# Expert gate tables: one-hot products on TensorE replaced by indirect adding transfers into zeroed device memory

## The reference, cut to what matters

```python
s1 = einsum('thd,hnd->thn', qp[..., :half], sub_k1)     # 8 heads, 128 keys each
s2 = einsum('thd,hnd->thn', qp[..., half:], sub_k2)
v1, i1 = top_k(s1, 16); v2, i2 = top_k(s2, 16)
vals, flat = top_k((v1[..., :, None] + v2[..., None, :]).reshape(T, 8, 256), 16)
experts = e1 * 128 + e2                                 # e1, e2: looked up in i1, i2 by flat
gates = softmax(vals)                                   # 16 per token and head
hid = gelu(einsum('cd,chkd->chk', x, u_tab[experts]))
out = einsum('chk,chkd->cd', gates * hid, v_tab[experts])
```

## Time and profile before

| | |
|---|---|
| median of 3 runs | 2321.66 us (2321.47 to 2322.29) |
| the profiled execution, span from first to last instruction | 2321.0 us |
| PE / DVE / ACT / POOL busy | 2284.5 / 1685.9 / 1213.7 / 475.5 us |
| granted TensorE clock, mean | 0.997 |
| mean DMA rate | 269 GB/s |

### The profile page before, as it was taken

The page is one execution under the profiler, slowest core; times in us unless marked ns, Lnnn a source line. Parts: engine busy times, 40 slices in busy tenths (PEclk is TensorE's granted clock), DMA queues, the critical chain, the costliest instruction groups (busy, mean ns, idle before and its releaser), DMA issues.

```text
span 2321.0 us, 36290 instructions
## 1 busy us (share of the span) xinstructions
PE 2284.5 (98%) x13406; PEld 2070.6 (89%) x13406; DVE 1685.9 (73%) x2063; ACT 1213.7 (52%) x1138; POOL 475.5 (20%) x430
## 2 busy tenths in 40 slices
PE   7999999999999999999999999999999999999997
PEld 6888888888888889999999999999999999899997
DVE  5544776556555555898899988887687888888765
ACT  5534555545454444566666656565544444444443
POOL 0001342000000000233444422212222222222000
PEclk9999999999999999999999999999999999999998
DMA  7755556544456656666666899998999999999882
GB/s 279 272 193 211 205 203 215 193 165 155 171 193 229 224 182 239 215 224 223 235 228 232 304 347 334 329 336 311 353 382 366 380 384 370 373 401 371 330 306 84
DMA packets 122281, 623.70 MB, mean 269 GB/s; under 512 B 12000, under 2 KB 40928, under 8 KB 61776
## 3 DMA queue, kind: packets, MB, share of 16 engines
q1 hardware_dynamic: 58752, 423.65, 49.9%
q0 software_dynamic: 25616, 156.65, 17.8%
q10 hardware_dynamic: 37824, 42.18, 5.1%
HBM read 576.29 MB, written 46.14 MB: 268 GB/s over the span
## 4 chain that ended last, share of the span: by engine, by line
PE 78%; DVE 13%; issue 6%; ACT 1%; DMA 1%; DVEq 0%; POOL 0%; ACTq 0%; SPq 0%; POOLq 0%
PE psum L1303 17%; PE psum L946 10%; PE psum L948 10%; PE psum L947 10%; PE psum L1254 9%; PE psum L1304 8%; PE psum L1255 4%; DVE w_lo L1391 4%; PE psum L1281 2%; PE psum L1080 1%; DVE s_now L1714 1%; DVE w_lo L1383 1%; PE psum L1002 1%; PE psum L1041 1%; DVE i_top L1700 1%
## 5 line engine op out<-in xcount | busy, mean ns | idle before, releaser
L1254 PE MATMUL psum<-h2T,w_hi 128*128 128x448 f32 x2048 | 645.8, 374 | 1.5 <-DVE w_lo L1391 1.5
L1303 PE MATMUL psum<-w_ul,w_hi 128*128 128x448 f32 x2048 | 643.1, 375 | 3.5 <-DVE w_ul L1801 3.5
L1255 PE MATMUL psum<-h2T,w_lo 128*128 128x224 f32 x2048 | 543.3, 265 | 0.0
L1304 PE MATMUL psum<-w_ul,w_lo 128*128 128x224 f32 x2048 | 540.9, 264 | 0.0
L1383 DVE TENSOR_TENSOR w_lo<-w_raw,w_hi 128x2048 fp32r<-128x2048 f32 x144 | 334.3, 2327 | 209.8 <-ACT w_hi L563 209.1
L1303 PEld LDWEIGHTS psum<-w_ul,w_hi 128*128 128x128 f32 x2048 | 384.1, 188 | 34.0 <-issue 4.2
L1254 PEld LDWEIGHTS psum<-h2T,w_hi 128*128 128x128 f32 x2048 | 383.8, 187 | 33.3 <-issue 3.5
L563 ACT ACTIVATE w_hi<-w_raw 128x2048 fp32r<-128x2048 f32 x144 | 275.5, 1913 | 253.3 <-DMA w_raw<-in_w_units 218.1
L1304 PEld LDWEIGHTS psum<-w_ul,w_lo 128*128 128x128 f32 x2048 | 390.7, 191 | 0.0
L1255 PEld LDWEIGHTS psum<-h2T,w_lo 128*128 128x128 f32 x2048 | 390.2, 191 | 0.0
L1391 DVE TENSOR_TENSOR w_lo<-w_raw,w_hi 128x2048 fp32r<-128x2048 f32 x128 | 295.5, 2310 | 66.1 <-ACT w_hi L575 63.4
(11 more groups left out here) (332 smaller groups left out, 2813.8 us busy)
## 6 DMA issues: line engine op xcount, KB each, us to landing
w_raw<-in_w_units SPq DMA_DIRECT2D x272, 1024.0 KB, 5.4
raw_x<-in_w_units SPq DMA_DIRECT2D x128, 1024.0 KB, 6.4
g_tab<-tab_scratch POOLq DMA_DIRECT2D x32, 896.0 KB, 8.8
h_in<-hid_scratch POOLq DMA_DIRECT2D x64, 448.0 KB, 6.1
hid_scratch<-hst ACTq DMA_DIRECT2D x32, 448.0 KB, 4.7
tab_scratch<-gate_a ACTq DMA_DIRECT2D x14, 1024.0 KB, 6.9
proj_scratch<-evac ACTq DMA_DIRECT2D x24, 512.0 KB, 4.7
x_nat<-in_x POOLq DMA_DIRECT2D x2, 2048.0 KB, 9.2
```

Of the source, the lines that this page charges most:

```text
L1254: pe.matmul(psum[:, k % 4, 0:2 * NU].rearrange("p (a t) -> p a t", a=2), uh, h2T[:, c, :, G:S], start=c == 0, stop=False, skip_group_check ...
L1255: ins = pe.matmul(psum[:, k % 4, NU:2 * NU], ul, h2T[:, c, 0, G:S], start=False, stop=c == KC - 1, skip_group_check=True)
L1303: pe.matmul(psum[:, c, 0:2 * NU].rearrange("p (a t) -> p a t", a=2), w_hi[:, s, o:o + P], ul, start=first, stop=False, skip_group_check=True)
L1304: return pe.matmul(psum[:, c, 0:NU], w_lo[:, s, o:o + P], ul[:, 0, :], start=False, stop=False, skip_group_check=True)
```

## The change

The gate table becomes one array in device memory, indexed by iteration, partition, expert in the group, and token. It is set to zero early: during the merge stage ACT's queue issues 16 stores of 0.9 MB from a tile of zeros. In the hidden stage POOL fills it by 256 indirect transfers (`scatter`): one for each route and pick, each adding one float per partition (96 or 128 floats) at an address held in `cells`. The address is worked out on DVE by four small instructions ahead of the lookup and one after it (`table_cells`). POOL's lookup now gives the whole address in one array.

After each group of four units POOL issues 7 of them while there is routing, 11 afterwards (`SCATTERED`). Before the first of each group of 16, POOL waits until all scatters so far have landed. The 27 gathers are issued in pairs ahead of the 11. In the last 8 iterations the sum of the two halves moves from POOL to DVE (`hidden_added`). DVE's copy of the scores into s_now goes away. `picks_hot`, `table`, `turn_picks`, `picks_out` and `table_out` go away, and with them 14 tables. The gathered tokens are now the last 32, so the tile with them is routed first. The rows of u and v are laid out in the new order by the host. PE's hidden loop becomes one loop; DVE's and POOL's become straight code. The diff, cut to its core:

```diff
+TG = 8
+ROWGAP = TG * (PEER_NK - 1)
+I_PICK, I_REST, I_END = 6, 8, 15
+PRE_SLOTS = [(I_REST + (2 * n + 5) // 8, (2 * n + 5) % 8) for n in range(PRE)]
+SCATTERS = ROUTES * TOPK
+SCATTERED = [min(7 * q, SCATTERS) if q < 2 * I_REST else min(7 * (2 * I_REST - 1) + 11 * (q - 2 * I_REST + 1), SCATTERS) for q in range(2 * U_IT)]
+def scattered_tokens(u):
+    return P - G if tile_of(u) == GT else P
...
@@ POOL
             def hidden_sum(m, q):
-                wait_alone(pool, hid_cross, m + 1)
+                pool.wait_ge(hid_cross, m + 1)
...
             def lookup(u):
+                pool.wait_ge(lookup_in, u + 1)
                 pool.tensor_tensor(hot[:, :, :, :], hot[:, :, :, :], if_top[:, :, None, :].to_broadcast([P, 2, TOPK, TOPK]), ALU.mult).then_inc(lookup_step, 1)
+                pool.wait_ge(lookup_step, u * 5 + 1)
+                pool.tensor_tensor(hot[:, 0, :, :], hot[:, 0, :, :], hot[:, 1, :, :], ALU.add).then_inc(lookup_step, 1)
                 for k, m in enumerate((8, 4, 2)):
+                    pool.wait_ge(lookup_step, u * 5 + k + 2)
+                    pool.tensor_tensor(hot[:, 0, :, 0:m], hot[:, 0, :, 0:m], hot[:, 0, :, m:2 * m], ALU.add).then_inc(lookup_step, 1)
...
+            def scatter(n):
+                u, k = n // TOPK, n % TOPK
+                tokens = scattered_tokens(u)
+                if n == 0:
+                    pool.wait_ge(tab_zeroed, 16 * U_IT)
+                if k == 0:
+                    pool.wait_ge(cells_done, u + 1)
+                    pool.wait_ge(routed, u + 1)
+                    if u:
+                        pool.wait_ge(tab_added, 16 * n)
+                pool.indirect_dma_start(tab_cells, bass.IndirectOffsetOnAxis(ap=cells[0:tokens, u, k:k + 1], axis=0),
+                                        rt[0:tokens, 1, u, k:k + 1], None, compute_op=ALU.add).then_inc(tab_added, 16)
...
-            with pool.Fori(0, I_TAB) as i:
+            for i in range(I_REST):
                 for j in range(4):
                     hidden_sum(i * 4 + j, j % 2)
                     if j % 2 == 1:
                         lookup(i * 2 + j // 2)
+                        scatters(i * 2 + j // 2)
...
-            for i in range(I_TAB, I_END):
+            for i in range(I_REST, U_IT):
                 for j in range(4):
-                    hidden_sum(i * 4 + j, j % 2)
-                    if (i - I_TAB) * 4 + j < PRE:
-                        gather((i - I_TAB) * 4 + j)
+                    if (i - I_REST) * 4 + j < PRE:
+                        gather((i - I_REST) * 4 + j)
+                    if j % 2 == 1:
+                        scatters(i * 2 + j // 2)
             pool.wait_ge(ring_used, PRE)
-            pool.wait_ge(tab_st, 16 * NTAB)
+            pool.wait_ge(tab_added, 16 * SCATTERS)
             v_tables(0)
@@ ACT
+            def zero_table(g):
+                if g == 0:
+                    act.wait_ge(zeros_done, 1)
+                act.dma_start(tab[g].rearrange("p (r n) -> p r n", n=2 * NU), zeros[:, None, :].to_broadcast([P, TG // 2, 2 * NU])).then_inc(tab_zeroed, 16)
-                    if k % 4 == 3 and tables:
-                        table_out(i * 2 + (k // 4 - 2 * I_TAB))
@@ PE
-                    if k % 4 == 2 and tables:
-                        table(i * 2 + (k // 4 - 2 * I_TAB))
@@ DVE
+            def table_cells(u):
+                t = tile_of(u)
+                dve.wait_ge(lookup_done, u + 1)
+                dve.tensor_scalar(cells[:, u, :], rt[:, 0, u, :], places[:, NT:NT + 1], places[:, t:t + 1], ALU.mult, ALU.add).then_inc(cells_done, 1)
...
-                    if part == 0:
-                        step(dve.tensor_copy(s_now[:, :, :].rearrange("p a n -> p (a n)"), sc[:, ds(u, 1), :].rearrange("p a n -> p (a n)")), alone=True)
-                    top16(s_now[:, part, :], s_cut[:, part, :], v_top[:, part, :], i_top[:, part, :])
+                    top16(sc[:, u, part * PEER_NK:(part + 1) * PEER_NK], s_cut[:, part, :], v_top[:, part, :], i_top[:, part, :])
...
+            def hidden_added(m):
+                dve.wait_ge(hid_cross, m + 1)
+                both = hs[:, m % 2, :, 0:NU]
+                dve.tensor_tensor(both, both, hs[:, m % 2, :, NU:2 * NU], ALU.add).then_inc(hid_added, 1)
-                        picks_hot(tb)
+                    if k % 2 == 1 and i >= I_REST:
+                        hidden_added(i * 4 + k // 2)
```

More of the change, by code:

```diff
@@ L62 @@
 PICKS = PEER_H * TOPK
-TB = 16
 G = 32
 NU = S - G
-TAB0 = G // TB
-NTAB = NU // TB
+GT = NT - 1
+TG = 8
+ROWGAP = TG * (PEER_NK - 1)
 RING = 3
@@ L76 @@
 BANK_ORDER = [0, 1, 4, 5, 2, 6, 3, 7]
+GT_FIRST = next(n for n in BANK_ORDER if n // 4 == GT)
 def chunk_count(h, c):
@@ L519, in _ @@
             v_load(1)
-            for m in range(4 * I_END + 1, 4 * U_IT):
-                hidden_sum(m, m % 2)
             pool.wait_ge(wlow_done, 1)
@@ L760, in _ @@
                     hi(n, n % 4)
+                    if k % 2 and 9 + b * 2 + k // 2 < U_IT:
+                        zero_table(9 + b * 2 + k // 2)
                 act.wait_ge(x1_done, b + 1)
@@ L835, in hidden_out, with hidden @@
                     act.dma_start(dst, hst[:, :]).then_inc(hid_st[half], 16)
-            def hidden(i, routes=False, tile=None, tables=False):
+            def hidden(i, routes=False):
                 for k in range(8):
@@ L868, in _ @@
             hidden(0, routes=True)
-            with act.Fori(1, I_PICK0) as i:
+            with act.Fori(1, I_REST) as i:
                 hidden(i, routes=True)
-            hidden(I_PICK0, routes=True, tile=0)
-            with act.Fori(I_PICK0 + 1, I_TAB) as i:
-                hidden(i, routes=True)
-            hidden(I_TAB, tables=True)
-            hidden(I_PICK1, tile=1, tables=True)
-            with act.Fori(I_PICK1 + 1, I_END) as i:
-                hidden(i, tables=True)
-            hidden(I_END)
+            for i in range(I_REST, U_IT):
+                hidden(i)
             hidden_out(U_IT - 1, 3)
@@ L1235, in _, with hidden @@
                         ins.then_inc(rs_row_done, 1)
-            def hidden(i, tile=None, tables=False):
+            def hidden(i):
                 for k in range(8):
@@ L1274, in table @@
-            def table(tb):
-                pe.wait_ge(hot1_done, tb + 1)
-                pe.wait_ge(hot2_done, tb + 1)
-                if not (isinstance(tb, int) and tb == 0):
-                    pe.wait_ge(tab_out, tb)
-                for j in range(TB):
-                    ins = pe.matmul(psum[:, 4 + j // 4, (j % 4) * P:(j % 4 + 1) * P], hot1a[:, j, :], hot2a[:, j, :], start=True, stop=True, skip_group_check=True)
-                ins.then_inc(tab_done, 1)
             pe.wait_ge(rs_row_out, 1)
@@ L1830, in _ @@
             dve.wait_ge(iota_in, 16)
+            dve.wait_ge(places_in, 16)
             dve.wait_ge(rs_row_out, 1)
             dve.wait_ge(sc_out, 2)
-            hidden(0, routes=True)
-            dve.wait_ge(sc_out, 4)
-            with dve.Fori(1, I_PICK0) as i:
-                step.enter(i, 1, 2 * ROUTE)
-                hidden(i, routes=True)
-                step.leave(I_PICK0 - 1)
-            for i in range(I_PICK0, I_TAB):
-                hidden(i, routes=True)
-            for i in range(I_TAB, I_END):
-                hidden(i, tables=True)
-            hidden(I_END)
+            for i in range(U_IT):
+                if i == 1:
+                    dve.wait_ge(sc_out, 4)
+                hidden(i)
             def experts_out(i, last=False):
@@ L1937, in _shape_constants @@
         "inv_f": inv.astype(np.float32)[None, :], "gla_masks": _gla_masks(),
-        "iota": np.arange(PEER_NK, dtype=np.float32)[None, :],
+        "iota": np.arange(TOPK, dtype=np.float32)[None, :],
+        "places": np.stack([*(np.arange(P) + t * P for t in range(NT)), np.full(P, NU)], axis=1).astype(np.float32),
     }
@@ L1956, in _layout @@
     v = a["peer_v"][0].reshape(PEER_NK, PEER_NK // 2, 2, 2, D // 2).transpose(3, 1, 0, 2, 4)
+    rows = [a[name][0].reshape(PEER_NK, U_IT, TG, D).transpose(1, 0, 2, 3).reshape(-1, D) for name in ("peer_u", "peer_v")]
     gla, nsa = _blocks(a["w_up_gla"][0]), _blocks(a["w_up_nsa"][0])
```

189 lines of the change are left out of this document (68 added, 121 removed).

## The result

| | before | after |
|---|---|---|
| median of 4 runs each, same chip | 2321.69 us (2321.47 to 2322.29) | 2458.82 us (2457.6 to 2460.07) |
| profiled execution, span | 2321.0 us | 2455.8 us |
| hidden stage, first hidden to first output matmul | 951.1 to 1651.9: 700.8 us | 950.5 to 1782.2: 831.7 us |
| output stage and end | 669.1 us | 673.6 us |

The change makes the kernel slower: 1.059 times the time before, 95% interval 1.0577 to 1.0603, 137 us. Of the 134.8 us between the spans the hidden stage holds 131. The predicted time was 2411 us with 2262 to 2500 around it.

The account below looks back on a forecast made before the run. PE, busy 98% of the span, was taken to bound the kernel before, POOL after the change. 2321.0 - 53 + 47 + 115 - 20 = 2410 us profiled, so 2411 us; range 2262 to 2500.

Parts of the forecast that it names:

- What the change takes away: Hidden stage, PE: 14 tables at 3.72 us, 52 us, plus some 1 us for six transposes: 53 us saved.
- What it adds away from POOL: DVE's address arithmetic and hidden_added, the 16 zeroing stores and the scatters' DMA traffic: claimed to cost nothing.
- A scatter: POOL, hidden stage: 1.28 us per scatter from start to start, taken from the gather of 128 addresses.
- Its wait under DVE: POOL's transfers beginning under two-operand DVE instructions wait for their end: 1.64 us lost per w_lo, 1.5 per gathered product.
- The landing: POOL's wait once in 16 scatters: 4 us, 1 of it under a w_lo; 1.3 and 2.1 us a group.
- The first half: Hidden-stage groups with routing, seven scatters each: 23.6 us against 20.45 before; 15 groups x 3.15 = 47 us.
- The second half: Hidden-stage groups with 11 scatters and 2 gathers: 28.3 us against PE's 19.94; 13.7 x 8.4 = 115 us.
- Slack: Work ahead in the first half and in the early gathers: 20 us spent before PE stops, taken off the sum.
- POOL keeps up: Rival: scatters at 0.65 us or less fit POOL's idle time and the 53 us are kept; 2262 to 2275, chance 0.22.
- the landing decides: Rival: landing takes 11.2 us as a gather's, groups 26.8 and 33.2 us; 2526 us, range 2500 to 2600, chance 0.12.
- it cancels: Rival: 1.0 us lost per DVE instruction, groups 21.0 and 24.7 us; 2323 us, no change, chance 0.02.
- The clock: Rival: with PE idle a fifth of the hidden stage its granted clock leaves full speed; far above 2500, chance 0.02.

Follow-up runs that it names:

- e1: The changed kernel with all 256 scatters and their landing waits left out: 2266.62 us, 0.9759 times the kernel before.
- e3: The changed kernel with scatters that write instead of adding (compute_op=ALU.add left out): 2374.38 us, 84 less than the changed kernel.
- e9: The changed kernel with 32 addresses in every scatter instead of 96 or 128, other tokens' gates left out: 2439.44 us, 19 less than the changed kernel.
- e5: The changed kernel with two zeroed gate tables filled in turn, so POOL waits only for the landing of the group before the last: 2420.53 us.
- e7: The changed kernel with the first half's sums moved from POOL to DVE too: 2430.55 us, 28 less than the changed kernel.
- e2: The changed kernel with every second scatter left out, 128 staying, and the same landing waits at the route borders: 2286.67 us.
- e4: The changed kernel with the hidden stage's w_lo made by a one-operand DVE instruction instead of a two-operand one: 2424.43 us, 34 less.

## Why the prediction was right, and where its sizes were off

The mechanism was the predicted one: POOL becomes the bound, with ACT waiting behind the scatters in the first half and DVE in the second. The sum was 46 us short, 2410 against 2455.8 in the profiled execution. The stated range of 2262 to 2500 says little by itself, since it held both signs; the narrower one of this case, 2330 to 2500, held the measurement too.

- **What the change takes away, 53 us.** e1 shows 54.7.
- **What it adds away from POOL, nothing.** e1 shows nothing: PE is busy in the whole stage. The output stage has 4.5 us more than before and 5.3 more than in e1, and these lie at its start. In its first 17.8 us PE issues 79 matmuls at a granted clock of 0.73, against 113 at 1.00 in e1; 34 matmuls at 0.156 us are 5.3 us.
- **A scatter, 1.28 us from start to start.** Too low. The gather was the wrong row for an addition: e3 shows 0.91 to 0.94 us for a write and 1.42 for an addition at the same 96 addresses. From start to start it is 1.72 and, with 128, 1.85. Each of seven in a group was about 0.45 short, each of eleven about 0.55 (by 23 of 96 and 128 of 128 addresses): 3 and 6 us a group. I had also argued that a gather's price is per address; for the adding transfers e9 shows that it is nearly all per instruction.
- **Its wait under DVE, 1.64 us for each w_lo and 1.5 for each product.** Too high in the second half, 9.6 us a group. With free scatters at 1.83 the group would be 11 x 1.83 + 2.6 = 22.7 us, and landing takes 2.5. 28.95 - 25.2 leaves 3.8 us. The phase isn't random, as I had assumed. POOL and DVE in the same moment, after:

```profile
1502.72 2.42 POOL L504 DMA_INDIRECT tab_scratch<-rt,cells  x1 [0.30 <-issue]
1505.44 1.91 POOL L504 DMA_INDIRECT tab_scratch<-rt,cells  x1 [0.30 <-issue]
1507.66 1.90 POOL L504 DMA_INDIRECT tab_scratch<-rt,cells  x1 [0.31 <-issue]
...
1503.64 2.29 DVE L1376 TENSOR_TENSOR w_lo<-raw_x,w_hi 128x2048 fp32r<-128x2048 f32 x1
1505.85 2.29 DVE L1376 TENSOR_TENSOR w_lo<-w_raw,w_hi 128x2048 fp32r<-128x2048 f32 x1
```

  The first scatter had waited for a product that ended at 1503.72; it ended 1.42 us after that, through the first half of a w_lo, and lost none by it. The second began under that w_lo, which ended at 1505.93, and ended 1.42 us later again, although the next w_lo had begun by then: it got in between. So where two-operand instructions follow each other one scatter passes for each, 2.2 us apart, and loses 0.35 us against its free 1.55, not 1.64. A queue that waits for such an instruction falls into step with it.
- **The landing, 3 us a wait beyond what is hidden.** 57.2 / 14 = 4.1 us; a group has 1.3 and 2.5 us of it, where I had 1.3 and 2.1. e5 takes the waits away and shortens the stage by 43.5 us. Landing itself, from the issue on, is 4.6 us at least and 7.1 in the median, not 4; part of it passes in other work. The Trainium skill's fixed 2.0 us (DMA: Bandwidth & Descriptors, Anatomy of one DMA — SWDGE path) is not seen: the quickest of the 256 took 4.6 us.
- **The first half, 23.6 us a group.** 24.68. The scatters with their gaps take 7 x (1.93 + 0.33) = 15.8 and landing 1.3; 7.6 is left for sums and lookup, where I had 6.4 before their waits. 15 x 1.08 = 16 us short. Another 8 us lie at its end: the last seven scatters stand between the last lookup and the first gather, 23.5 us against 15.9 before, and the 15 periods don't hold them. I had also read POOL as idle in three quarters of this half, where the earlier trace rows has it busy for 143.5 of 344.5 us, so idle in 58%; no term of the sum hangs on that.
- **The second half, 28.3 us.** 28.95, right in size for a wrong reason: the transfer was 6 us a group dearer, and its wait 5.8 cheaper. 13.7 x 0.65 = 9 us short.
- **Slack, 20 us.** About right, but its counterpart at the end was left out. From the start of the last gather PE needs 28.4 us to its last hidden matmul (1748.2 to 1776.6), where before it needed 50.5 us with one table in them, and in e1 45.7 us (1551.8 to 1597.5). So 17 to 18 us of work ahead were spent. Then PE stands still for 5.6 us, which it did not before, when it passed from one stage to the other in 0.3 us:

```profile
1776.38 0.26 PE L1274 MATMUL psum<-h2T,w_lo 128*128 128x224 f32 x1
1782.21 0.71 PE L1288 MATMUL psum<-w_ul,w_hi 128*128 128x448 f32 x1 [5.57 <-DVE w_lo L1376]
```

  What it stands still for, by the chain that ended last (start, us, what):

```profile
1762.29 2.43 POOL tab_scratch L504
...
1765.02 4.39 DMA tab_scratch<-rt,cells
...
1769.98 0.60 POOL g_tab L475
1770.58 5.30 DMA h_in<-hid_scratch
...
1775.91 1.10 DVE h_in L1773
...
1777.03 0.02 ACT w_ul L891
```

  The landing of the last scatter, the tables' load behind it, the product; then ACT's w_hi, DVE's w_lo and PE's first output matmul at 1782.2, 17 us after the last scatter was issued. The first 11.6 of these 17 us pass beside PE's last hidden units.
- **The rivals.** That POOL keeps up is out: no scatter is under 1.4 us. That the landing decides is out: e5 without its waits is at 2420. That it cancels is out. The clock did fall, see below; the second-half group is accounted for by POOL alone, so its price lies beside POOL's.
- **The signs.** POOL was to be busy in over 85% of the hidden stage and is busy in 78% (646.9 of 831.7 us); the rest is the 0.30 us ahead of each scatter and the waits for landing. DVE was to wait for the lookup in the first half; ACT, which waits for the sums on the same list, comes to its wait first, and DVE stands behind ACT's w_hi. Only in e7, without that wait, does DVE wait for the lookup.

In all, the sum was 24 us short in the first half (16 + 8), some 10 in the second, 7 in the slack (5.6 of them PE's stand at the end) and 4.5 in the output stage: the 46 us between the sum and the span. The terms that were most off in size are the price of a scatter (1.28 against 1.72 and 1.85 us) and, the other way, its wait under DVE in the second half. That the two nearly cancelled in the second half was luck; without it the sum would have missed by far more.

## What to carry to other kernels

Before work goes to an idle engine, count its instructions, not its bytes: 256 transfers of half a kilobyte cost 1.7 to 1.9 us of issue each, and replaced 14 tables at 3.72 us. An idle share of an engine is a stock that can be filled at a small price (e2: 128 scatters for 20 us, 0.16 us each) and beyond which each instruction costs a large part of its length (e2 to after: 1.34 us each, of 2.2 with its gap). A step whose results the next stage reads at once must end early enough for the landing and the next load, or its tail stands on the path whatever slack there was ahead of it (5.6 us here).

## What the runs showed of the hardware

- An indirect transfer that adds takes 0.5 us longer to issue than one that writes (1.42 against 0.91 to 0.94, 96 addresses). Its price hardly depends on the number of addresses: 1.31, 1.42 and 1.55 us for 32, 96 and 128.
- A free gather of 1 MB and a free write of 384 bytes take the same 0.9 to 1.0 us on POOL.
- An indirect transfer that begins under a DVE instruction with two operands ends a fixed time after it, 1.3 us with 96 addresses and 1.42 with 128 when it adds (112 of 112), 0.77 to 0.89 when it writes (113 of 113, e3), and also when the next such instruction has begun by then. One that is under way when such an instruction begins is not held. Under DVE's one-operand w_lo one that is under way is held as well, to 0.07 to 0.12 us after it (58 of 72, e4).
- The granted clock fell as PE began to wait, to 0.87 in the second half. PE in the timeline near the end of the stage, before and after a wait for w_lo:

```profile
1751.26 0.38 PE L1273 MATMUL psum<-h2T,w_hi 128*128 128x448 f32 x1
1751.47 0.26 PE L1274 MATMUL psum<-h2T,w_lo 128*128 128x224 f32 x1
1758.50 0.71 PE L1273 MATMUL psum<-h2T,w_hi 128*128 128x448 f32 x1 [6.77 <-DVE w_lo L1376]
1759.02 0.39 PE L1274 MATMUL psum<-h2T,w_lo 128*128 128x224 f32 x1
1759.20 0.60 PE L1273 MATMUL psum<-h2T,w_hi 128*128 128x448 f32 x1
```

  After 6.8 us of standing still a pair of matmuls takes 0.59 us instead of 0.31, the lower of the two levels, 1.2 GHz. In e1, where PE never waits in this stage, the clock is 1.00. PE had time to spare in these groups, so I read the lower clock as a symptom of the waits, not their cause; no run held the clock up with the waits in place.
